# A fused transformer stack: the mixer's output product is begun between its last rounds, and the attentions turn their weights one step later

## The reference

```python
s = (jnp.einsum('bhqd,bhkd->bhqk', qc, k) * scale + cq[..., None] - cum[:, :, None, :])
p = masked_softmax(s, key_pos[None, :] <= t[:, None])
return jnp.einsum('bhqk,bhkd->bhqd', p, v)
...
attn = diff_attention(q, k, v, lam, attn_subln_g, lambda_init)   # 8 heads, two softmaxes each
ssm = ssd_mixer(z, xbc, dt, conv_w, conv_b, dt_bias, a_log, d_skip, ssm_norm_g)
mixed = jnp.concatenate([attn, ssm], axis=-1) @ w_out             # 1536 x 1024
x = x + rms_norm(mixed, mix_post_g)
```

## Time and profile before

| | us |
|---|---|
| median of three runs | 1268.11 (1267.1 to 1269.16) |
| the profiled execution | 1271.67 |
| its span, first to last instruction | 1269.8 |
| PE busy in the span | 1202.0 (95%) |
| DVE busy | 834.7 (66%) |
| ACT busy | 652.7 (51%) |
| POOL busy | 236.0 (19%) |

### The profile page before, as it was taken

One profiled execution on the slowest core, in us unless ns is written; L12 is line 12 of the kernel. 1 busy time (PEld: TensorE's weight loads), 2 busy tenths in 40 slices (PEclk: granted clock), 3 DMA queues, 4 the chain that ended last, 5 costly groups with the idle time before them and its releaser, 6 DMA issues.

```text
span 1269.8 us, 19077 instructions
## 1 busy us (share of the span) xinstructions
PE 1202.0 (95%) x7698; PEld 1046.5 (82%) x7698; DVE 834.7 (66%) x1291; ACT 652.7 (51%) x1060; POOL 236.0 (19%) x300
## 2 busy tenths in 40 slices
PE   6898899999999889999999999999998789999996
PEld 5785588888888668888888889999996479888996
DVE  6955586666586567666557876457866856776643
ACT  6436566644333656664446555346545545655531
POOL 4103331110000232111112212000005510111101
PEclk9999999999999999999999999999999789999998
DMA  7790155564453424545554554652441023455461
GB/s 277 263 213 34 39 194 177 188 219 179 168 191 137 167 95 175 194 173 197 199 199 138 194 199 147 206 212 103 167 173 50 1 108 134 174 190 192 147 203 56
DMA packets 34088, 205.56 MB, mean 162 GB/s; under 512 B 3776, under 2 KB 6352, under 8 KB 13776
## 3 DMA queue, kind: packets, MB, share of 16 engines
q1 hardware_dynamic: 30704, 200.47, 44.3%
q10 hardware_dynamic: 3296, 3.87, 1.6%
HBM read 202.87 MB, written 1.46 MB: 161 GB/s over the span
## 4 chain that ended last, share of the span: by engine, by line
PE 79%; DVE 14%; ACT 3%; POOL 2%; issue 1%; DMA 1%; POOLq 0%; ACTq 0%; DVEq 0%
PE ps L662 36%; PE ps L667 23%; PE ps L665 5%; PE ps L666 5%; DVE wl L604 3%; PE ps L686 1%; PE ps L687 1%; PE ps L688 1%; DVE tf L2181 1%; POOL pb L965 1%; PE ps L909 1%; DVE y L1932 1%; DVE xb L740 1%; PE ps L1420 1%; ACT wh L575 1%
## 5 line engine op out<-in xcount | busy, mean ns | idle before, releaser
L604 DVE TENSOR_TENSOR wl<-raw,wh 128x2048 fp32r<-128x2048 f32 (+4 forms) x196 | 421.2, 2154 | 149.7 <-ACT wh L575 149.6
L662 PE MATMUL ps<-xb,wh 128*128 128x512 f32 x1424 | 502.8, 398 | 4.2 <-DVE wl L604 3.7
L667 PE MATMUL ps<-xb,wl 128*128 128x256 f32 x1696 | 477.1, 281 | 0.0
L575 ACT ACTIVATE wh<-raw 128x2048 fp32r<-128x2048 f32 (+4 forms) x196 | 348.5, 1781 | 153.3 <-PE ps L667 119.2
L662 PEld LDWEIGHTS ps<-xb,wh 128*128 128x128 f32 x1424 | 267.3, 188 | 70.5 <-issue 5.4
L667 PEld LDWEIGHTS ps<-xb,wl 128*128 128x128 f32 x1696 | 321.9, 190 | 0.0
L667 PE MATMUL ps<-ab,wl 128*128 128x256 f32 x1088 | 307.4, 283 | 0.0
L662 PE MATMUL ps<-ab,wh 128*128 128x512 f32 x640 | 226.8, 400 | 0.8 <-DVE ab L975 0.8
L667 PEld LDWEIGHTS ps<-ab,wl 128*128 128x128 f32 x1088 | 207.3, 191 | 0.0
L662 PEld LDWEIGHTS ps<-ab,wh 128*128 128x128 f32 x640 | 120.3, 188 | 31.7 <-DVE ab L975 1.4
L859 DVE TENSOR_TENSOR tf<-ps,tf 128x256 f32<-128x256 f32 x148 | 61.9, 421 | 119.6 <-ACT tf L854 119.6
(11 more groups left out here) (322 smaller groups left out, 1332.1 us busy)
## 6 DMA issues: line engine op xcount, KB each, us to landing
raw<-wstream SPq DMA_DIRECT2D x156, 1024.0 KB, 4.8
raw<-wstream SPq DMA_DIRECT2D x32, 704.0 KB, 4.0
raw<-wstream SPq DMA_DIRECT2D x8, 768.0 KB, 4.1
e_bt<-scratch ACTq DMA_DIRECT2D x16, 128.0 KB, 8.6
o_bt<-scratch SPq DMA_DIRECT2D x2, 1024.0 KB, 9.9
raw<-wstream SPq DMA_DIRECT2D x2, 560.0 KB, 7.2
raw<-wstream SPq DMA_DIRECT2D x4, 256.0 KB, 6.7
h<-xt ACTq DMA_DIRECT2D x4, 256.0 KB, 7.8
```

What stands on the lines that cost most here:

```text
L575: e.g.activation(WH[i % HLN][:, 0:w], RAW[i % RAWN][:, 0:w], ACT.Copy).then_inc(S["hi"], 1)
L604: e.g.tensor_tensor(WL[q][:, 0:w], RAW[i % RAWN][:, 0:w], f32(WH[q][:, 0:w]), ALU.subtract).then_inc(S["lo"], 1)
L662: e.g.matmul(PS[b][:, :].rearrange("p (a t) -> p a t", a=2), wh[:, sl], x2[:, :, cs], start=start, stop=k == p.nk - 1, skip_group_check=pair)
L667: ins = e.g.matmul(o, wl[:, sl], xh[:, cs], start=False, stop=k == p.nk - 1, skip_group_check=pair)
```

## The change

There are two parts.

**The attentions.** Turn, copy of the turned weights and value product all come one iteration later: in iteration i PE turns step i-3, at odd i it does the value product of steps i-5 and i-4, and the loops have one more iteration. Which engine copies a step stays the same (ACT even steps, DVE odd steps). On DVE the copy of step q now stands behind the maximum of step q+3 and the reciprocal of step q+2.

**The mixer.**
- `mo` is in 6 chunks of 16 blocks. The first three hold all 12 k of n = 0 to 3, k by k; the last three hold n = 4 to 7. It writes to PSUM banks 3, 4 (n = 0 to 3), 0, 1, 2, which the norms don't use, and the next product begins in banks 5 and 6.
- PE issues the 48 blocks of n = 0 to 3 between the rounds' own work (`begun`): tiles k = 4, 5, 0 in round 7, 6 and 7 in round 8, 1 in round 9, 8 and 9 in round 10, 2 in round 11, 10, 11 and 3 in round 12. The other 48 blocks follow behind the rounds.
- On DVE the norm steps stand behind the combining of the round's weights instead of ahead of it. The reading of the norm sums with the epsilon (`nb_a`) moves from DVE to ACT (`first_factor`: logarithm straight from PSUM, an Identity with the bias, exponential). On PE the `sub` sums come behind decay and state products.
- ACT splits chunk 2 of `mo` in round 0 and chunk 3 at the end of round 10; DVE does a quarter of chunk 2 in each of rounds 1 to 4 and two quarters of chunk 3 in each of rounds 11 and 12.
- POOL's `weighted` runs two pairs ahead instead of one, ahead of `gated`.

```diff
-    cols("w_out_2", 0, tiles(0, 8), MIXK, 12)
+    half = [("w_out_2", 0, k * 128, n * 128, 128) for k in MIXK for n in range(4)]
+    half += [("w_out_2", 0, k * 128, n * 128, 128) for n in range(4, 8) for k in MIXK]
+    for i in range(0, len(half), 16):
+        chunks.append(half[i:i + 16])
...
-        Gemm("mo", "cols", 8, 12, 12, "pg"),
-        Gemm("gate2", "cols", 2 * F2, 8, 16, "ev_dve", kmajor=4, after=6, fixed=(3, 4), wide=True),
+        Gemm("mo", "cols", 8, 12, 16, "pg", kmajor=4, fixed=(3, 4, 0, 1, 2)),
+        Gemm("gate2", "cols", 2 * F2, 8, 16, "ev_dve", kmajor=4, after=6, fixed=(5, 6, 0, 1, 2, 3, 4), wide=True),
...
             A = ODD
-            for i in range(A.n + 3):
+            for i in range(A.n + 4):
                 if i % 2 and i + 1 < A.n:
                     pe_odd_scores(e, i + 1)
-                if 0 <= i - 2 < A.n:
...
-                    pe_turn(e, A, i - 2)
-                q = i - 4
-                if i % 2 == 0 and 0 <= q < A.n:
+                if 0 <= i - 3 < A.n:
...
+                    pe_turn(e, A, i - 3)
+                q = i - 5
+                if i % 2 and 0 <= q < A.n:
...
+            def first_factor(e, no, a, o):
+
+                e.wait_ge(S["nb_m"], no)
+                e.wait_ge(S["eps"], 1)
+                e.link(e.g.activation(o, PS[NB][:, 0:T], ACT.Ln, bias=EPS[:, 1:2]))
+                e.g.activation(a, PS[NB][:, 0:T], ACT.Identity, bias=EPS[:, 1:2]).then_inc(S["nb_a"], 1)
+                e.settle()
+                e.g.activation(o, o, ACT.Exp, scale=-0.5).then_inc(S["nb_y"], 1)
...
             weighted(0)
+            weighted(1)
             gated(0)
             A = MIX
             for i in range(ROUNDS):
-                if i + 1 < 8:
-                    weighted(i + 1)
...
+                if i + 2 < 8:
+                    weighted(i + 2)
                 if i + 1 < 8:
                     gated(i + 1)
...
+                if 1 <= i <= 4:
+                    lo_part(e, G["mo"].first + 2, i - 1)
+                if i >= 11:
+                    lo_part(e, G["mo"].first + 3, 2 * i - 22)
+                    lo_part(e, G["mo"].first + 3, 2 * i - 21)
...
+            def begun(*tiles):
+
+                for t in tiles:
+                    at = 4 * MIXK.index(t)
+                    pe_cols(e, G["mo"], MIXK, AB, ready, part=slice(at, at + 4))
...
+                if i == 7:
+                    begun(4)
                 if i % 2 and 0 <= i - 3 < 8:
                     pe_mixer_pv(e, (i - 3) // 2)
                 if i % 4 == 3 and i < 8:
                     e.wait_ge(S["gq"], i + 1)
                     pe_sums(e, "ones512", (ACC, ACC2)[i // 4][:, :], nb_no("grp", i // 4))
...
+                begun(*{7: (5, 0), 8: (6, 7), 9: (1,), 10: (8, 9), 11: (2,), 12: (10, 11, 3)}.get(i, ()))
+            pe_cols(e, G["mo"], MIXK, AB, ready, part=slice(48, None))
```

More of the change, by code:

```diff
@@ L240, in __init__ @@
                 order += [(n, k, n // 2, 2 * k + n if name == "r" else n % 2 * nk + k) for k in range(nk) for n in range(n0)]
+            elif kmajor:
+                n0 = kmajor
+                order += [(n, k, (k * n0 + n) // per, (k * n0 + n) % per) for k in range(nk) for n in range(n0)]
             elif per == nk:
@@ L641, in pe_chunk, with pe_cols @@
             return WH[c % HLN], WL[c % HLN]
-        def pe_cols(e, p, ks, xb, ready, after=None):
+        def pe_cols(e, p, ks, xb, ready, after=None, part=slice(None)):
             x2 = xb[:, :].rearrange("p (a t) -> p a t", a=2)
@@ L649, in pe_cols @@
             done = 0
-            for n, k, c, at, fresh, signals in p.blocks:
+            for n, k, c, at, fresh, signals in p.blocks[part]:
                 b = p.bank[p.unit(n)]
@@ L1264, in dve_even @@
             A = EVEN
-            for i in range(A.n + 4):
+            for i in range(A.n + 5):
                 if i == 2:
@@ L1381, in pe_even @@
             pe_even_scores(e, 0)
[L1382 removed]
+            for i in range(A.n + 4):
                 if i == 2:
                     pe_toks(e, G["ev1"], x_ready(0))
[L1385 removed]
+                if i == 12:
                     e.wait_ge(S["ol"], 3)
@@ L1685, in pe_odd @@
             pe_odd_scores(e, 0)
-            for i in range(A.n + 3):
+            for i in range(A.n + 4):
                 if i % 2 and i + 1 < A.n:
                     pe_odd_scores(e, i + 1)
-                if 0 <= i - 2 < A.n:
-                    if i - 2 < 2:
-                        e.wait(G["odd"].free.get(A.turn_bank(i - 2)))
-                    pe_turn(e, A, i - 2)
-                q = i - 4
-                if i % 2 == 0 and 0 <= q < A.n:
+                if 0 <= i - 3 < A.n:
+                    if i - 3 < 2:
+                        e.wait(G["odd"].free.get(A.turn_bank(i - 3)))
+                    pe_turn(e, A, i - 3)
+                q = i - 5
+                if i % 2 and 0 <= q < A.n:
                     d = q // 2
@@ L1980, in pe_idle @@
             wh, _ = pe_chunk(e, p.first + p.chunks)
-            o = PS[3]
-            e.wait(G["mu" if at == 0 else "gate2"].free[0])
+            to = G["mu" if at == 0 else "gate2"]
+            o = PS[to.bank[0]]
+            e.wait(to.free[0])
             for i in range(36):
@@ L2103, in act_mixer @@
                     act_turned(e, A, 2 * (i - 1) + 1)
+                for kind, s, step in late_steps(i):
+                    if (kind, step) == ("grp", 1):
+                        if s:
+                            e.wait_ge(S["yn"], 4 * s)
+                        first_factor(e, nb_no("grp", s), TMP[1][:, 0:T], RB[:, 0:T])
                 if i + 2 < 8:
                     act_decay(e, i + 2)
+                if i == 0:
+                    hi_to(e, G["mo"].first + 2)
                 s = (i - 3) // 2
```

121 lines of the change are left out of this document (56 added, 65 removed).

## The result

The changed kernel takes **1252.12 us** (median of 4 runs, 1251.94 to 1254.83) against 1268.18 us for the kernel before in the same session (1267.1 to 1269.16). The ratio is 0.9879, 95% interval 0.9861 to 0.9896: 16 us less, where 20 were forecast. The profiled execution took 1254.83 us; its span is 1253.0 us against 1269.8.

What follows compares the result with a forecast made beforehand. A latency loop bounds the attentions, and DVE's norm work ahead of the weights holds up the mixer. Mixer 12, even attention 5 and odd 3.5 sum to 20.5 us off 1268.1: 1248 us, range 1240 to 1259.

Steps and rivals of the forecast that it cites:

- the ring: Attentions: turn, DVE copy, maximum and POOL scaling wait on each other, 4.04 us a pair, with no engine full.
- I cost them at nothing: Odd attention's end: last turn, copy and value product come an iteration later, no ACT or DVE work between, no cost.
- start and end together: Even attention: longer start, freeing DVE's long first wait, and longer drain at the end, together put at +0.3 us.
- its old distance: Mixer: the last turn was taken to stay at 1015.79, unchanged in distance from the end of round 5.
- the norm steps gone from ahead of the weights give 4 us earlier weights: Mixer, DVE: low parts, Newton step and scaling over two rounds no longer delay the weights, 4 us.
- 0, from -2 to +2: Mixer's early rounds: chunk 2 quarters and POOL's decay matrices ahead were taken to cancel, 0 us within that range.
- The earlier weights pay for the blocks: Mixer: 12 blocks ahead of the last turn (4.3 us full clock, 7.9 half) are offset by 4 us earlier weights.
- C: Rival, 10%: mixer blocks ahead of the turn run at half clock or await low parts; mixer gives 4 to 6, 1254 to 1256.
- granted clock near 1.0: Sign in the mixer's rounds: clock near full in the stretch that had 0.58; staying at 0.5 would favour C.
- A: Rival, 15%: the attentions give nothing, the period stays at 4 us; the mixer's 12 alone gives 1256.
- B: Rival, 15%: full clock through the mixer's rounds, turn 4 us earlier, attention waits nearly gone; 26 us, 1242.
- D: Rival, 4%: slower; attention maximum waits for a younger turn, four buffers too few, 6.4 us a pair, 1296.

Runs made afterwards that it cites:

- the maxima first: Changed kernel with the next round's row maxima and DVE's decay matrix put ahead of the round's norm steps on DVE: 1254.66 us, ratio 0.9887.
- all three: Changed kernel with next-round maxima ahead of DVE's norm steps, ACT's high parts behind the exponentials, chunk 2 quarters in rounds 7 to 10: 1251.45 us, ratio 0.9849.
- both queues opened: Kernel with the maxima first, plus ACT's high parts of rounds 5 to 7 moved behind the next round's exponentials: 1250.04 us, ratio 0.9857.
- POOL one pair ahead: Changed kernel with POOL's decay matrices one pair ahead, as in the kernel before, instead of two: 1251.13 us, ratio 0.9852.

## Why the prediction was right, and where it was not

The time lies in the range and the sign and the order of size are right; 20.5 us were summed up and 16 measured. Most of what is missing is in the mixer, 9.6 us between its marks for 12. By its own terms:

**The odd attention: 3.5 forecast, 2.6 measured.** The mechanism is shown by the trace: the ring is open and the fullest engine sets the period, which was worked out as 3.62, 3.54, 3.34 and 3.34 and came as 3.17 to 3.59. The term that was wrong is the end: "I cost them at nothing". The drain got 1.1 us longer (8.86 to 9.94). The reason given, that nothing of ACT or DVE stands between the moved steps, was false, since an exponential stands there; but with that taken away 0.8 of the 1.1 us are still there.

**The even attention: 5 forecast, 4.6 measured** (5.4 from its first scores). The nine pairs came as worked out, 29.4 us against 30.2. The drain cost 1.3 us (8.85 to 10.11) where start and end together had been put at +0.3.

**From the last turn to the product's end: 33.8 forecast, 34.0 measured** (1010.47 to 1044.49; 45.4 before). The 84 blocks, the two sums and the value product at full clock and one wait of 1.5 us: that wait is there, 1.40 us, for ACT's reading of the norm sum:

```profile
1012.36 0.67 PE L2421 MATMUL ps<-tmp,consts 128*128 128x256 f32 x2 [1.40 <-ACT tmp L2087]
```

**The last turn: forecast at its old distance, measured 1.8 us later** (55.7 us behind the first state product, before 53.9). Two steps failed here. First, "the norm steps gone from ahead of the weights give 4 us earlier weights": the turn of round 6, which needs the weights of round 5, did come 4.3 us earlier, and the next round gave it all back, since on DVE and on ACT the norm work stood ahead of the maxima and the exponentials. With the norm steps put back the total stays as it is. I had asked what stood behind the weights, and not what stood behind the norm steps in their new place. Second, the quarters and POOL's order, "0, from -2 to +2": moved to rounds 7 to 10 the quarters gave 2.8 us in one pair of profiles, 1.6 and 0.8 in two others, and the last turn came 3.1, 1.8 and 2.0 us earlier. The prediction had also worked out 9 us for the mixer if all quarters and the moved norm steps met POOL, and 9.6 were measured. But contention as such is only part of it: three quarters were 0.53 us longer each, and in round 5 the three steps from 991.16 took 0.83, 0.83 and 0.72 beside POOL where the same three took 0.42, 0.43 and 0.42 right behind them.

**The begun blocks.** "The earlier weights pay for the blocks" was not what happened; the blocks delay the last turn by 2.9 us. But they are worth it by more than was counted, 5.3 us net: without them the wait for ACT behind the turn is 2.2 us longer, and the clock falls once more.

Of the rivals, C is the nearest: the clock did fall in the later rounds, to a mean of 0.74. Its place was another, between the turns of rounds 6 and 7 and ahead of the blocks, and its price was 2.4 us of the mixer's 12 and not 6 to 8. The sign "granted clock near 1.0" did not come: it was 0.50 from 995.6 to 1005.8. A didn't come: the attentions gave 7.2 us by the marks, and B didn't, since the turn came no earlier. D didn't come: the maximum never waited for a turn in the odd attention, and in the even one only once, for 6.7 us at the start, where before DVE had waited 8.0; so four buffers are enough at this depth.

## What to carry to other kernels

When work that is not urgent is moved behind something urgent in an in-order queue, look at what it is now ahead of: in a loop, behind this round's result is ahead of the next round's input. Follow it on every engine that passes the work on; here DVE's steps and ACT's steps that wait for them closed two queues at the same moment, and opening one showed nothing. The same holds for a result brought forward: it is worth only as much as what follows it doesn't wait for another queue, as the 3.55 us behind the earlier last turn show. A filler is worth most on an engine whose clock falls when it is idle, and least in a round that has no slack; and small fillers are not placed by counting idle time alone, but by what the neighbouring engine reads at that moment.

## What the runs showed of the hardware

PE came back at half clock from its idle stretches in the later rounds (5.9 us in the changed kernel, 4.8 with the maxima first, 3.9 with all three), and blocks ran at 0.64 us instead of 0.36. In the changed kernel the granted clock was 0.50 from 995.6 to 1005.84, and PE was busy for all of the 7.87 us from its return at 997.97: I estimate from this that the wait of 5.9 us cost about 3.9 us more behind it. A long wait isn't the only thing ahead of which the clock fell. In the changed kernel it was at 0.50 from 985.36 to 988.77 with PE busy throughout and one wait of 0.99 us ahead of it, and in the kernel with both queues opened from 987.1 to 1000.8 with no wait over 1.6 us. Neither can I explain.

Less expected: PE's pace at a granted clock of 1.00 is not the same in all executions. Two profiles of the same code, in the same stretch, with PE busy throughout (the columns as in the earlier trace rows). First the changed kernel, then the one with POOL one pair ahead, which is the same up to the mixer:

```profile
180.00:220.00 40.00, 40.00 (x228) 34.66 (x227) 24.83 (x29) 25.55 (x37) 7.28 (x7) 1.00 0.53 184
```

```profile
180.00:220.00 40.00, 40.00 (x233) 35.24 (x232) 25.17 (x29) 25.63 (x36) 8.02 (x8) 1.00 0.52 184
```

233 matmuls against 228 in 40 us, a difference of 2%. Records missing from one trace don't explain it: both hold 7698 matmuls, and those of 512 columns in this stretch took 399 ns on the mean in the first and 391 in the second. By 415 us the second execution was 4.5 us ahead, though nothing had been changed there, and its total shows it; why it was faster is open. Runs of one kernel spread over 5 us and more on these chips (the kernel before from 1262.97 to 1271.97 in one session). That is why the experiments are read between marks.
